# Weighing the values of two attention heads in turn, and one key projection for two heads

## The reference, cut to what matters

```python
q = jnp.einsum('bsc,chd->bshd', rmsnorm(cq, P['mla_q_norm']), P['mla_w_uq'])
s = (jnp.einsum('bqhc,bkc->bhqk', qlb, ckv)
     + jnp.einsum('bqhr,bkr->bhqk', qrb, kr)).astype(jnp.float32) * MLA_SCALE
s = jnp.where(key_chunk[None, :] <= q_chunk[:, None], s, -jnp.inf)
pr = jax.nn.softmax(s, axis=-1).astype(ckv.dtype)
o_lat = jnp.einsum('bhqk,bkc->bqhc', pr, ckv)
y_mla = jnp.einsum('bshc,chv->bshv', o_lat, P['mla_w_uv']).reshape(B, S, MLA_WIDTH)
```

## Time and profile before

| | us |
|---|---|
| median of 3 runs (lowest, highest) | 1958.69 (1958.23, 1962.24) |
| the profiled execution's own time | 1959.1 |
| its span in the profile | 1957.3 |
| TensorE busy (matmuls) | 1844.1 |
| VectorE busy | 1021.1 |
| ScalarE busy | 727.9 |
| GpSimd busy | 105.2 |
| the two woven stretches (166 to 334, 1128 to 1296) | 168 each |

### The profile page before, as it was taken

One profiled execution on the slowest core, in us unless ns is written; L12 is line 12 of the kernel. 1 busy time (PEld: TensorE's weight loads), 2 busy tenths in 40 slices (PEclk: granted clock), 3 DMA queues, 4 the chain that ended last, 5 costly groups with the idle time before them and its releaser, 6 DMA issues.

```text
span 1957.3 us, 37713 instructions
## 1 busy us (share of the span) xinstructions
PE 1844.1 (94%) x16582; PEld 1708.6 (87%) x16582; DVE 1021.1 (52%) x1741; ACT 727.9 (37%) x1292; POOL 105.2 (5%) x108
## 2 busy tenths in 40 slices
PE   6988998999999999999999799989998999999997
PEld 5975776999699999999999577779986999999997
DVE  6777665554335534343357765655443455353533
ACT  4435546463334222121335355454433422121212
POOL 2010000200010000000100100001000200000001
PEclk9998999999999999999999799999998999999998
DMA  6100000553022222222221000123510222232221
GB/s 226 65 8 1 4 23 26 192 175 115 29 65 87 87 87 87 92 82 97 83 80 44 8 3 3 34 99 123 201 46 30 76 87 94 80 97 84 90 87 57
DMA packets 38595, 149.53 MB, mean 76 GB/s; under 512 B 4384, under 2 KB 4544, under 8 KB 36768
## 3 DMA queue, kind: packets, MB, share of 16 engines
q1 hardware_dynamic: 36288, 131.05, 20.2%
q0 software_dynamic: 2144, 16.06, 2.2%
HBM read 139.68 MB, written 7.41 MB: 75 GB/s over the span
## 4 chain that ended last, share of the span: by engine, by line
PE 87%; DVE 6%; ACT 4%; issue 1%; DMA 1%; POOL 1%; DVEq 0%; SPq 0%; ACTq 0%; POOLq 0%
PE PS L605 79%; PE PS L730 6%; PE PS L969 1%; ACT hH L1096 1%; POOL sq L531 1%; DVE rs L1840 0%; PE PS L1065 0%; DVE stat L1868 0%; DVE hT L1839 0%; DMA ring<-wall 0%; ACT sq L1096 0%; ACT L1096 0%; DVE hL L1521 0%; DVE kf L1699 0%; POOL msq L583 0%
## 5 line engine op out<-in xcount | busy, mean ns | idle before, releaser
L605 PE MATMUL PS<-hH,wH 128*128 128x272 f32 x2272 | 488.4, 297 | 31.1 <-DMA cst<-cst_in 16.3
L605 PE MATMUL PS<-hH,wL 128*128 128x272 f32 x2272 | 477.0, 291 | 0.0
L605 PE MATMUL PS<-hL,wH 128*128 128x272 f32 x2272 | 476.2, 291 | 0.0
L1512 DVE TENSOR_TENSOR wL<-ring,wH 128x1024 fp32r<-128x1024 f32 x238 | 301.0, 1266 | 216.3 <-ACT wH L1096 215.9
L605 PEld LDWEIGHTS PS<-hH,wH 128*128 128x128 f32 x2272 | 361.6, 191 | 43.8 <-issue 20.7
L1096 ACT ACTIVATE wH<-ring 128x1024 fp32r<-128x1024 f32 x238 | 249.8, 1051 | 334.4 <-PE PS L605 328.6
L605 PEld LDWEIGHTS PS<-hH,wL 128*128 128x128 f32 x2272 | 362.6, 191 | 0.0
L605 PEld LDWEIGHTS PS<-hL,wH 128*128 128x128 f32 x2272 | 360.5, 191 | 0.0
L605 PE MATMUL PS<-hidH,wL 128*128 128x272 f32 x1024 | 212.0, 288 | 0.0
L605 PE MATMUL PS<-hidH,wH 128*128 128x272 f32 x1024 | 211.7, 288 | 0.0
L605 PE MATMUL PS<-hidL,wH 128*128 128x272 f32 x1024 | 211.1, 288 | 0.0
(11 more groups left out here) (307 smaller groups left out, 2543.5 us busy)
## 6 DMA issues: line engine op xcount, KB each, us to landing
ring<-wall SPq DMA_DIRECT2D x238, 512.0 KB, 3.3
lw<-lw_in POOLq DMA_DIRECT2D x2, 2240.0 KB, 10.2
xT<-x_in SPq DMA_DIRECT2D x4, 544.0 KB, 6.6
y_out<-hT SPq DMA_DIRECT2D x8, 272.0 KB, 2.1
mem<-mem_in POOLq DMA_DIRECT2D x2, 1024.0 KB, 5.2
mks<-mks_in POOLq DMA_DIRECT2D x2, 1024.0 KB, 10.7
mvs<-mvs_in POOLq DMA_DIRECT2D x2, 1024.0 KB, 13.6
memk_out<-mkp POOLq DMA_DIRECT2D x2, 1024.0 KB, 6.8
```

Of the source, the lines that this page charges most:

```text
L605: return e.matmul(out, lhsT=a, rhs=b, start=start, stop=stop)
L1512: tt(wL[:, n % SPLIT], ring[:, n % RING], plain(wH[:, n % SPLIT]), ALU.subtract).then_inc(w_lo, 1)
```

## The change

Three things are done together.

**Weighing by pairs.** `weigh` runs for the units of odd heads alone and does both heads of the pair there: for each key block j the even head's product (columns 0 to 63 of the array, since its result goes to partitions 0 to 63), then the odd head's (columns 64 to 127). The number of products stays. The transposed probabilities of an even head must live five units longer, so `turned(u)` gives them buffers of their own (`aPTf`, `odd_turned`, and parts of the small weights `uv` and `wa` that are no longer needed), those of the sample now packed into 96 columns. `head_out` runs for odd heads and copies 128 partitions at once (20 copies a layer in place of 40).

**One key projection for two heads.** `project` with p = 2 and 3 runs for even heads alone, with 128 stationary columns of `uk` (two heads). `keys_hi` then copies the upper 64 partitions to a buffer (`keys_kept`, semaphore `k_kept`); for the odd head both `keys_hi` and `keys_lo` read that buffer. `wait_bank` after a key projection waits for `k_kept` too.

**Waits.** `keys_hi` for an even head from 2 on waits for `k_out` of the head before, before it overwrites the kept keys. `norm_early(2)` waits for its own engine's `gn_var`. `USES` and the counts follow.

```diff
@@ -110,8 +110,12 @@
-    USES += [("s", _u)] + [("w", _u - 2)] * (_u > 1)
-    if _h + 1 < HEADS and _b < 4:
+    USES.append(("s", _u))
+    if _u > 1 and UNITS[_u - 2][0] % 2:
+        USES.append(("w", _u - 2))
+    if _h + 1 < HEADS and _b < (2 if _h % 2 == 0 else 4):
@@ -211,8 +215,8 @@
-    "q_out": 2 * HEADS, "k_mm": 2 * HEADS, "k_hi": 2 * HEADS, "k_out": 2 * HEADS,
-    "a_score": 40, "a_max": 40, "a_exp": 40, "a_norm": 40, "a_T": 40, "a_T_out": 40, "a_pv": 40, "a_o": 40,
+    "q_out": 2 * HEADS, "k_mm": HEADS, "k_kept": HEADS, "k_hi": 2 * HEADS, "k_out": 2 * HEADS,
+    "a_score": 40, "a_max": 40, "a_exp": 40, "a_norm": 40, "a_T": 40, "a_T_out": 40, "a_pv": 20, "a_o": 20,
@@ -275,6 +279,13 @@
+        aPTf, = carve(col["aPT"], ARENA, aPTf=(1024,))
+        odd_turned, = carve(col["kk"] + 512, col["cq"], odd_turned=(384,))
+        k_prompt, = carve(col["xs"] + 2 * FR, col["kk"], k_prompt=(SEQ,))
+        k_others, = carve(col["rg"] + 792, col["gate"] + 64, k_others=(KEYS - SEQ,))
@@ -387,6 +398,26 @@
+        def turned(u):
+            h, b = UNITS[u]
+            n = 128 * b + 128 if b < 4 else 3 * DEC
+            if h % 2:
+                return W("wa", 0, n) if b % 2 else odd_turned[:, 0:n]
+            if b == 3:
+                return W("uv", 0, n)
+            at_ = (0, 128, 384, 0, 768)[b]
+            return aPTf[:, at_:at_ + n]
+        def keys_kept(h, p):
+            if p == 3:
+                return k_others[0:64, :]
+            return W("wa", 0, SEQ, rows_of[0]) if h < 2 else k_prompt[0:64, :]
+        def weighed_no(u):
+            h, b = UNITS[u]
+            return 5 * (h // 2) + b + 1
         def values(j):
@@ -402,7 +433,7 @@
-                e.wait_ge(s["a_o"], at(l, "a_o", n + 1))
+                e.wait_ge(s["a_o"], at(l, "a_o", weighed_no(n)))
@@ -410,6 +441,7 @@
+                e.wait_ge(s["k_kept"], at(l, "k_kept", n // 4 + n % 4 - 1))
         def weave(recurrence, attention):
@@ -933,10 +965,10 @@
-                        mm(o[0:64, :], W("uk", 64 * h, 64 * h + 64), ckv[:, 0:SEQ]).then_inc(s["k_mm"], 1)
+                        mm(o, W("uk", 64 * h, 64 * h + 128), ckv[:, 0:SEQ]).then_inc(s["k_mm"], 1)
-                        mm(o[0:64, 0:DEC], W("uk", 64 * h, 64 * h + 64), ckv[:, SEQ:T])
-                        mm(o[0:64, DEC:DEC + PAST], W("uk", 64 * h, 64 * h + 64),
+                        mm(o[:, 0:DEC], W("uk", 64 * h, 64 * h + 128), ckv[:, SEQ:T])
+                        mm(o[:, DEC:DEC + PAST], W("uk", 64 * h, 64 * h + 128),
                 def score(u):
@@ -981,18 +1013,18 @@
-                    rows = rows_of[h % 2]
+                    heads = ((h - 1, turned(u - 5)), (h, turned(u)))
-                        o = weighed(128)[rows, :]
-                            last = mm(o, values(j)[:, 64 * h:64 * h + 64], aPT[:, u % 2, 128 * j:128 * j + 128],
-                                      j == 0, j == b)
+                            for i, m in heads:
+                                last = mm(weighed(128)[rows_of[i % 2], :], values(j)[:, 64 * i:64 * i + 64],
+                                          m[:, 128 * j:128 * j + 128], j == 0, j == b)
-                        o = weighed(DEC)[rows, :]
-                        mm(o, values(4)[0:DEC, 64 * h:64 * h + 64], aPT[0:DEC, u % 2, 0:DEC], True, False)
-                        for j in range(2):
-                            last = mm(o, values(5 + j)[:, 64 * h:64 * h + 64],
-                                      aPT[:, u % 2, 128 * j + 128:128 * j + 128 + DEC], False, j == 1)
+                        for j in range(3):
+                            for i, m in heads:
+                                r = slice(0, 128) if j else slice(0, DEC)
+                                last = mm(weighed(DEC)[rows_of[i % 2], :], values(4 + j)[r, 64 * i:64 * i + 64],
+                                          m[r, DEC * j:DEC * j + DEC], j == 0, j == 2)
                 def attention():
@@ -1003,10 +1035,10 @@
-                        if u >= 2:
+                        if u >= 2 and UNITS[u - 2][0] % 2:
-                        if h + 1 < HEADS and b < 4:
+                        if h + 1 < HEADS and b < (2 if h % 2 == 0 else 4):
@@ -1277,6 +1309,7 @@
+                        e.wait_ge(s["gn_var"], at(l, "gn_var"))
@@ -1318,29 +1351,33 @@
-                    e.wait_ge(s["k_mm"], at(l, "k_mm", 2 * h + p - 1))
-                    act(akH[0:64, h % 2, a:b], bank(bank_of(("p", n)), 0, b - a)[0:64, :],
-                        ACT.Copy).then_inc(s["k_hi"], 1)
+                    if h % 2:
+                        e.wait_ge(s["k_kept"], at(l, "k_kept", h - 1 + p - 1))
+                        act(akH[0:64, 1, a:b], keys_kept(h - 1, p), ACT.Copy).then_inc(s["k_hi"], 1)
+                        return
+                    e.wait_ge(s["k_mm"], at(l, "k_mm", h + p - 1))
+                    o = bank(bank_of(("p", n)), 0, b - a)
+                    act(akH[0:64, 0, a:b], o[0:64, :], ACT.Copy).then_inc(s["k_hi"], 1)
+                    if h:
+                        e.wait_ge(s["k_out"], at(l, "k_out", 2 * h))
+                    act(keys_kept(h, p), o[64:128, :], ACT.Copy).then_inc(s["k_kept"], 1)
                 def turned_out(u):
-                        last = act(aPT[:, u % 2, 0:128 * b + 128], bank(6, 0, 128 * b + 128), ACT.Copy)
+                        last = act(turned(u), bank(6, 0, 128 * b + 128), ACT.Copy)
-                        act(aPT[0:DEC, u % 2, 0:DEC], bank(6, 0, DEC)[0:DEC, :], ACT.Copy)
-                        last = act(pair(aPT[:, u % 2, 128:384])[:, :, 0:DEC],
-                                   pair(bank(6, 128, 384))[:, :, 0:DEC], ACT.Copy)
+                        act(turned(u)[0:DEC, 0:DEC], bank(6, 0, DEC)[0:DEC, :], ACT.Copy)
+                        last = act(pair(turned(u)[:, DEC:3 * DEC]), pair(bank(6, 128, 384))[:, :, 0:DEC], ACT.Copy)
                 def head_out(u):
-                    e.wait_ge(s["a_pv"], at(l, "a_pv", u + 1))
-                    rows = rows_of[h % 2]
-                    act(hT[rows, 4 + h // 2, 128 * b:128 * b + n], weighed(n)[rows, :],
-                        ACT.Copy).then_inc(s["a_o"], 1)
+                    e.wait_ge(s["a_pv"], at(l, "a_pv", weighed_no(u)))
+                    act(hT[:, 4 + h // 2, 128 * b:128 * b + n], weighed(n), ACT.Copy).then_inc(s["a_o"], 1)
                 def attention():
@@ -1859,8 +1896,13 @@
-                    tt(akL(l, h % 2)[0:64, a:b], bank(bank_of(("p", n)), 0, b - a)[0:64, :],
-                       plain(akH[0:64, h % 2, a:b]), ALU.subtract).then_inc(s["k_out"], 1)
+                    if h % 2:
+                        e.wait_ge(s["k_kept"], at(l, "k_kept", h - 1 + p - 1))
+                        whole = keys_kept(h - 1, p)
+                    else:
+                        whole = bank(bank_of(("p", n)), 0, b - a)[0:64, :]
+                    tt(akL(l, h % 2)[0:64, a:b], whole, plain(akH[0:64, h % 2, a:b]),
+                       ALU.subtract).then_inc(s["k_out"], 1)
                 def maximum(u, name, n, nk, scale, scores):
```

## The result

The changed kernel takes **1950.03 us** (median of 19 runs, 1945.05 to 1956.73), the kernel before on the same chips 1958.76 (19 runs, 1956.05 to 1964.86). The ratio is 0.9949, 95% interval 0.9940 to 0.9959: faster by 0.5%, 8.7 us. The forecast was 1925, range 1910 to 1945. The direction was right, the size was not, and the time lies outside the range.

What follows compares the result with a forecast made beforehand. TensorE's queue was taken to bound the woven stretch from 166 us, VectorE the piece before. Savings of 20.4 us a layer less 3.6 given back make 16.8, 33.6 for two layers: 1925 us from 1959.1, range 1910 to 1945.

Steps and rivals of the forecast that it cites:

- weighings 9.9 and projections 5.1: Per layer, separate weighings of heads 2, 4, 6 save 9.9 us, key projections of heads 3, 5, 7 save 5.1.
- the clock, at 0 in the sum: Woven stretch: TensorE's granted clock was to stay 1.00, so the sum holds no clock loss.
- case D: Even heads 2, 4, 6: 84% busy TensorE gets the lower clock, 34.8 us a layer lost, 2029 us; chance 0.04.
- Head 0's weighings and head 1's second projection: Only the work behind 166 us counts: 2.4 us a layer for head 0, 0.7 us for head 1.
- VectorE's stretch: From 140 to 166 us VectorE's work on the factors sets the length; shorter TensorE work there saves nothing.
- The 2.3 us of waits: TensorE idles 4.6 us ahead of weighings; with half the visits gone, 2.3 us a layer is saved.
- Full overlap of the halves: Odd heads' paired visits: both column halves run in the time of one, 0.055 us an instruction instead of 0.11.
- Case B: Odd heads' visits: the halves take turns, 11.0 us a layer paid again, 1947 us; chance 0.12.
- What comes back: Even heads: thinner TensorE work exposes waits for VectorE and ScalarE, 3.6 us a layer, bounds 0 and 7.2.
- ScalarE's copies at nothing: ScalarE's new kept-key copies in three heads cost 0, bounds 0 and 3 us a layer; 20 copies are dropped.
- 140 to 166 us keep their length: The piece ahead of the woven stretch, set by VectorE, keeps its 26 us.
- The woven stretch of 147 to 155 us: The stretch that began at 166 us, 168 us long before, was to last 147 to 155 us in both layers.

Runs made afterwards that it cites:

- x1: Changed kernel with pair weighing and shared key projection only from head 2 on, heads 0 and 1 as before the change: 1938.21 us, ratio 0.9898 to the kernel before.
- x13: x9 with three more TensorE waits, one in head 4 and two in head 7, filled with unread products: 1936.08 us, ratio 0.9871 to the kernel before.
- x9: Changed kernel with six unread products in unit 4, where head 0's weighing of block 2 stood: 1940.28 us, ratio 0.9898 to the kernel before.
- x5: Changed kernel with pair weighing only from head 2 on, shared key projection from head 0 on: 1943.28 us, ratio 0.9908 to the kernel before.
- x6: Changed kernel with pair weighing from head 0 on, shared key projection only from head 2 on: 1942.79 us, ratio 0.9901 to the kernel before.
- x3: Kernel before the change without head 0's weighings and their copies, its part of the output left stale: 1958.9 us, ratio 0.9983 to the kernel before.
- x8: x1 with ScalarE's copies of the kept keys moved behind its copy of the transposed probabilities: 1943.98 us, ratio 0.9915 to the kernel before.
- x2: Changed kernel with the first score matmul repeated in units 2 to 6, results overwritten: 1954.17 us, ratio 0.9966 to the kernel before.
- x10: Changed kernel with fifteen unread products of 256 columns in TensorE's wait for the factors: 1946.55 us, ratio 0.9923 to the kernel before.
- x7: x1 with all products of a pair's even head ahead of those of the odd head: 1944.04 us, ratio 0.9914 to the kernel before.

## Why the prediction was wrong, and where it was right

Per layer, in us. "Clock kept" is the first layer of x1 for heads 2 to 7 and of x13 for heads 0 and 1; x13 has the same length in heads 2 to 7.

| term | forecast | clock kept | changed kernel |
|---|---|---|---|
| heads 2 to 7: TensorE's work, weighings 9.9 and projections 5.1 | 15.0 | 14.9 | |
| idle time of TensorE: 2.3 saved ahead of weighings, 3.6 given back | -1.3 | -3.8 | |
| heads 0 and 1: 2.4 and 0.7 | 3.1 | 1.3 | |
| clock | 0 | | -8.5 |
| sum | 16.8 | 12.4 | 3.9 |

The first two rows are read from heads 2 to 7 of the first layer, the kernel before and then x1, both at the upper level with nothing filled:

```profile
188.31:333.87 145.56, 134.72 (x2416) 107.08 (x2412) 84.97 (x252) 74.53 (x208) 1.15 (x2) 1.00 0.04 14
190.16:324.63 134.47, 119.83 (x2398) 99.28 (x2394) 84.30 (x252) 71.73 (x197) 1.16 (x2) 1.00 0.05 15
```

- **The step that failed: the clock, at 0 in the sum, and case D's bound on it.** It is 8.5 of the 12.9 us a layer by which the forecast was too high. Case D had the mechanism, at 0.04, but tied it to the even heads' average of 84% busy, where it does not occur: heads 2 and 4 have 1.00. In heads 0 and 1 it fell at one hole, which costs 0.5 and 5.3 us and is shown by x9. Its falls in head 7 cost 2.7 us more (together 183.6 against 175.1); that they too come from holes is likely and not shown. An average over a head cannot show a hole of 1.5 us. The row was there to be had: the step behind head 0's weighing of block 2 begins the moment VectorE's "P" is done. The prediction counted that weighing as a gain of 0.80 us and did not ask what ended at its end. It took head 1's second key projection going as well: x5 and x6, each with one of the two, keep the clock.
- **Head 0's weighings and head 1's second projection.** The same step: work up to 170 us is in front of a wait for VectorE, so the border of "VectorE's stretch" is not at 166 us. 1.3 us came of 3.1, the clock kept; x3 gives 1.7 for the weighings of all of head 0 alone.
- **The 2.3 us of waits: too much.** The idle time ahead of weighings was to be halved with the visits. Groups by form, 166 to 334 us, first a form of the kernel before that the earlier trace rows does not show, then the forms of the changed kernel that waited:

```profile
L605 PE MATMUL PS<-aPT,av 32*64 32x32 f32 x16 | 2.3, 221 | 1.5 <-DVE rs L1840 1.0 <-ACT hT L1096 0.5
L637 PE MATMUL PS<-aPTf,av 128*64 128x128 f32 x48 | 8.0, 291 | 3.6 <-ACT lw L1128 1.6 <-DVE bonus L1842 1.1 <-ACT odd_turned L1128 0.8
L637 PE MATMUL PS<-aPTf,av 32*64 32x32 f32 x8 | 1.1, 217 | 1.2 <-DVE rs L1877 0.7 <-ACT hT L1128 0.5
```

  That is 4.6 + 1.5 = 6.1 us before and 4.8 now: 1.3 us less there, while all idle time of TensorE in heads 2 to 7 grew by 3.8. Where another engine ends the wait, taking away the instruction that waited does not end it sooner, as the hole at 168.6 us shows.
- **Full overlap of the halves: right.** The visit of 16 instructions takes 1.02 us to the next row (forecast 1.0 to 1.2):

```profile
194.46 1.09 PE L637 MATMUL PS<-lw,av 128*64 128x128 f32 x16
195.48 0.68 PE L762 MATMUL PS<-XX,LG 64*64 64x64 f32 x8
```

  The Trainium skill (TensorE: Matmul & The Clock Gate, section Part 3: Packing small matmuls) has weight loads overlap only between row groups; here both halves use all rows, and the measurement decides against it: 16 instructions with their loads take the 1.02 us that 8 took. Case B is out.
- **What comes back: near, but not to be told apart from the waits.** The two idle terms made -1.3 us together and measured -3.8 in heads 2 to 7; with the 1.3 us saved ahead of weighings, about 5 us came back for the 3.6 forecast, within its bounds of 0 and 7.2. TensorE's idle share is 5.7% in head 2 and 13.1% in head 4, within the 5 to 16% named. In head 4 it is a wait of 1.5 us for ScalarE's "TK", of the sort named as late next.
- **ScalarE's copies at nothing: right** (x8). **140 to 166 us keep their length: right**; TensorE's work there fell by 3.9 us and nothing came of it: head 0 takes 24.6 us for 24.3.
- **The woven stretch of 147 to 155 us: wrong.** With the clock kept the heads are 12.4 us shorter, in the changed kernel 3.9 and 3.7.
- With the clock kept in all heads the table gives 1959.1 - 2 x 12.4 = 1934.3, and x13 measured 1934.64 to 1939.87, within the forecast's range, as x1 and x9 are. In x13's profiled execution (1939.87) the heads are 23.2 us shorter and the other stages 4 us longer. How many late falls an execution has varies too; the changed kernel's runs go from 1945.05 us (mean clock 0.967) to 1956.73 (0.960).

Open is what decides whether a given hole brings a fall, and how long the fall lasts. It is not the hole alone: x6 has the early one and no fall, x1 has the changed kernel's head 7 and no fall there, and x3 has the old head 7 and falls in both layers.

## What to carry to other kernels

Before you remove TensorE work that stands in front of a wait for another engine, look at what ends when it ends: if the wait ends at the same moment, the removal buys nothing and leaves a hole, and the clock can fall at the hole and cost several times the work removed (here 0.80 and 0.69 us of work removed ahead of the wait, 5.8 us lost in heads 0 and 1). Read the granted clock by head or finer, not by stage, before and after. Where such a hole can't be avoided, keep the old form for that head (x1) or put unread products into it (x9), no longer than the wait.

## What was not expected of the hardware

- TensorE was busy 16.98 of 17.40 us from 170 us on, at the lower level throughout (windows above). Once down, full work did not bring the clock back for 17 us. In x2 and x10 the fall at this place lasted 10.2 and 3.4 us.
- Column halves fed by the same rows run side by side, in pairs 0.01 us apart (changed kernel, TensorE's timeline):

```profile
326.05 0.27 PE L637 MATMUL PS<-aPTf,av 128*64 128x128 f32 x1
326.06 0.27 PE L637 MATMUL PS<-odd_turned,av 128*64 128x128 f32 x1
326.16 0.27 PE L637 MATMUL PS<-aPTf,av 128*64 128x128 f32 x1
326.17 0.27 PE L637 MATMUL PS<-odd_turned,av 128*64 128x128 f32 x1
```

- Even in x7, where the program has all of one half first, 16 instructions take 1.51 us, and not the 1.9 that 16 x 0.11 + 0.14 would give: in the trace the starts fall into two series of eight, each with 0.11 us steps after the first, from 276.94 and from 277.44 us, so the second half begins with three matmuls of the first still to start.
